# Conformer and differential attention trunk: PSUM banks, weight splits and read-backs of the attention stage

## What is computed

```python
q = (h @ w_q).reshape(B, S, N_HEADS, 2, HEAD_DIM)       # 8 heads, two halves of 64
for i in range(S // Q_BLOCK):                           # 8 query blocks of 128 rows
    end = (i + 1) * Q_BLOCK
    s = jnp.einsum("bqhcd,bkhcd->bhcqk", q_blk, k_pre) * scale
    p = jax.nn.softmax(s + bias[None, :, None], axis=-1)
    attn = p[:, :, 0] - lam * p[:, :, 1]
    outs.append(jnp.einsum("bhqk,bkhe->bqhe", attn, v_pre))
o = rmsnorm(o, subln_g) * (1.0 - lambda_init)
return o.reshape(B, S, V_WIDTH) @ w_o
```

## Time and profile before

| | |
|---|---|
| median of 3 runs | 2633.22 us (2631.69 to 2634.12) |
| profiled execution, its own time | 2629.98 us |
| its span | 2628.2 us |
| granted TensorE clock, mean | 0.972 |
| PE busy | 2425.7 us (92%) |
| DVE busy | 1477.3 us (56%) |
| ACT busy | 785.7 us (30%) |
| chain that ended last | PE 79%, DVE 15%, ACT 3% |

### The profile page before, as it was taken

How to read it: one execution, slowest core, us unless ns; L and a number is a source line. 1 busy time by engine, 2 the same in 40 slices (tenths; PEclk the granted TensorE clock), 3 DMA queues, 4 the chain that set the end, 5 groups by cost and what they waited for, 6 DMA issues and landing times.

```text
span 2628.2 us, 26809 instructions
## 1 busy us (share of the span) xinstructions
PE 2425.7 (92%) x10851; PEld 1929.7 (73%) x10851; DVE 1477.3 (56%) x2204; ACT 785.7 (30%) x1204; POOL 62.1 (2%) x51
## 2 busy tenths in 40 slices
PE   7995899999999999988888888679999999999997
PEld 5883688887777888866666666458688888888885
DVE  6998499895545344446766766653533333333233
ACT  5211432223434222234444444331421121121113
POOL 0000000000000000010111010000000000000000
PEclk9997899999999999999999999889999999999998
DMA  3110233332323333310111100211111111111111
GB/s 125 41 49 16 64 88 97 94 95 88 94 81 86 98 97 96 99 29 21 33 32 33 33 29 17 62 45 53 32 47 44 56 44 45 56 44 45 56 32 65
DMA packets 278297, 155.14 MB, mean 59 GB/s; under 512 B 5701, under 2 KB 273310, under 8 KB 278174
## 3 DMA queue, kind: packets, MB, share of 16 engines
q1 hardware_dynamic: 278174, 153.42, 19.6%
HBM read 145.54 MB, written 7.86 MB: 58 GB/s over the span
## 4 chain that ended last, share of the span: by engine, by line
PE 79%; DVE 15%; ACT 3%; issue 2%; DMA 1%; SPq 0%; DVEq 0%; ACTq 0%
PE ps L1333 25%; PE ps L1335 25%; PE ps L1334 24%; PE ps L1392 3%; DVE cacc L945 2%; DVE cvA L945 2%; PE ps L1316 2%; DVE rb L1182 1%; DVE sc L1161 1%; ACT sc L744 1%; DVE Wl L1107 1%; DVE sc L1159 1%; ACT ATh L757 1%; DVE sc L1146 1%; DVE Wl L873 1%
## 5 line engine op out<-in xcount | busy, mean ns | idle before, releaser
L1333 PE MATMUL ps<-Sh,Wl 128*128 128x512 f32 x2304 | 946.5, 411 | 87.3 <-DVE kS L1129 35.5
L1335 PE MATMUL ps<-Sh,Wh 128*128 128x512 f32 x2304 | 909.2, 395 | 0.0
L1334 PE MATMUL ps<-Sl,Wh 128*128 128x512 f32 x2304 | 908.6, 394 | 0.0
L1333 PEld LDWEIGHTS ps<-Sh,Wl 128*128 128x128 f32 x2304 | 439.0, 191 | 213.3 <-issue 105.5
L1335 PEld LDWEIGHTS ps<-Sh,Wh 128*128 128x128 f32 x2304 | 438.7, 190 | 94.6
L1334 PEld LDWEIGHTS ps<-Sl,Wh 128*128 128x128 f32 x2304 | 439.4, 191 | 93.5 <-issue 10.6
L873 DVE TENSOR_TENSOR Wl<-raw,Wh 128x1024 fp32r<-128x1024 f32 (+3 forms) x246 | 285.6, 1161 | 132.0 <-ACT Wh L566 130.9
L566 ACT ACTIVATE Wh<-raw 128x1024 fp32r<-128x1024 f32 (+3 forms) x246 | 245.7, 1002 | 321.2 <-PE ps L1335 159.7
L1057 DVE TENSOR_TENSOR xT<-ps,xT 128x512 f32<-128x512 f32 x112 | 77.2, 689 | 241.9 <-PE ps L1335 241.9
L757 ACT ACTIVATE ATh<-ps 128x512 fp32r<-128x512 f32 (+2 forms) x96 | 47.0, 489 | 311.8 <-PE ps L1316 311.7
L1050 DVE TENSOR_TENSOR tmp<-ps,rstd 128x512 f32<-128x512 f32 x66 | 45.6, 691 | 167.4 <-PE ps L1335 167.4
(11 more groups left out here) (161 smaller groups left out, 2686.0 us busy)
## 6 DMA issues: line engine op xcount, KB each, us to landing
raw<-in_ffn_w_dram SPq DMA_DIRECT2D x148, 512.0 KB, 3.8
raw<-in_pw_w_dram SPq DMA_DIRECT2D x32, 512.0 KB, 3.7
raw<-in_ffn_w_dram SPq DMA_DIRECT2D x32, 448.0 KB, 3.4
raw<-in_ffn_w_dram SPq DMA_DIRECT2D x24, 384.0 KB, 3.2
xrow<-in_x_dram SPq DMA_DIRECT2D x8, 512.0 KB, 7.6
raw<-in_w_q_dram SPq DMA_DIRECT2D x8, 512.0 KB, 3.7
raw<-in_w_k_dram SPq DMA_DIRECT2D x8, 512.0 KB, 3.8
raw<-in_w_v_dram SPq DMA_DIRECT2D x8, 512.0 KB, 3.6
```

The lines of the kernel that those rows point to most:

```text
L1333: pe.matmul(dst, ll, rh, start=start, stop=False)
L1334: pe.matmul(dst, lh, rl, start=False, stop=False)
L1335: return pe.matmul(dst, lh, rh, start=False, stop=stop)
```

## The change

Four things. The six projections of a head, and in head 7 the first seven output products, alternate between banks 0 and 1; each waits for the one two before it. All turns (transposes of weights and of V, sums of squares) go through bank 6, each waits for the one before it. Weight blocks are split one slot earlier: K and V of head h + 1 in rows 0 and 2, Q of head h + 2 in row 5, and Q of head 1 before the first scores. The read-back of results goes into `oback`, which lies exactly where `Sl` lies, so that no transfer waits for a buffer and the low part is written in place; the transfers begin when the last projection is done.

```diff
-TURN_BANKS = (6, 1)
+def row_parts(h, i):
+    table = LAST_FILL if h == HEADS - 1 else FILL
+    u = sum(map(sum, table[:i]))
+    for part in range(4):
+        if part == 1:
+            if i == 5:
+                yield ("o", h, 0), 0, 1
+            yield ("w", h, i, 0), 0, 1
+        if part == 2 and i < 2:
+            yield ("v", h, i), 0, 1
+        if part == 3:
+            if i == 0 and h:
+                yield ("o", h - 1, 1), 0, 1
+            if i >= 4:
+                yield ("w", h, i, 1), 0, 1
+        for n in range(table[i][part]):
+            yield projection(h, u)
+            u += 1
...
+def plan():
+    bank, before, holder = {}, {}, {0: None, 1: None, 6: None}
+    turn = 0
+    for key, step, _ in through_banks():
+        if step == 0:
+            bank[key] = 6
+            if key[0] in "pr":
+                bank[key] = turn % 2
+                turn += 1
+            before[key] = holder[bank[key]]
+            holder[bank[key]] = key
+    return bank, before
...
-        ostage = [qS, kS]
+        oback = at("oback", [P, 2, KC, HT], F32, S_AT + 32 * KB)
...
                 if h == HEADS - 1:
+                    sp.wait_ge(pj_mm, 6 * HEADS)
                     for k in range(HEADS - 1):
-
                         sp.wait_ge(o_out, 32 * (k + 1))
-                        if k < 2:
-                            sp.wait_ge(qk_lo, 4 * HEADS)
-                        else:
-                            sp.wait_ge(o_lo, k - 1)
-                        sp.dma_start(ostage[k % 2][:, :], o_dram[k]).then_inc(o_in[k % 2], 16)
+                        sp.dma_start(oback[:, :, k, :], o_dram[k].rearrange("p (a b) -> p a b", b=HT)) \
+                            .then_inc(o_in[k], 16)
...
                 if not last:
-                    if i in (0, 2, 4):
-                        att_split(h + 1, i // 2)
+                    if i in (0, 2):
+                        att_split(h + 1, K_R + i // 2)
+                    if i == 5 and h < HEADS - 2:
+                        att_split(h + 2, Q_R)
...
             att_split(0, V_R)
+            att_split(1, Q_R)
...
+            def bank_free(key):
+                b = BEFORE[key]
+                if b is None:
+                    pe.wait_ge(add_ok, 6 * KC)
+                elif b[0] == "p":
+                    pe.wait_ge(pj_ev, 6 * b[1] + (FIRST_ORDER.index(b[2]) if b[1] == 0 and b[2] < 4 else b[2]) + 1)
+                elif b[0] == "o":
+                    pe.wait_ge(ostd_ok, 2 * b[1] + b[2] + 1)
+                elif b[0] == "r":
+                    pe.wait_ge(wo_ev, b[1] + 1)
+                else:
+                    pe.wait_ge(tr_ev, SPLIT_TURN[b] + 1)
```

More of the change, by code:

```diff
@@ L145, with projection, through_banks @@
 LAST_DONE = [sum(map(sum, LAST_FILL[1:i + 1])) // (HEADS - 1) for i in range(TB)]
-def turns():
+MORDER = (5, 0, 1, 2, 3, 4)
+def projection(h, u):
+    if h == HEADS - 1 and u >= KC:
+        return ("r", (u - KC) // (HEADS - 1)), (u - KC) % (HEADS - 1), HEADS - 1
+    return ("p", h + (u >= KC), MORDER[u // KC]), u % KC, KC
+def row_parts(h, i):
[16 more added lines that the diff above has]
+            u += 1
+def through_banks():
+    for m in (0, 2, 1, 3, 4):
+        yield ("p", 0, m), 0, 1
     for h in range(HEADS):
         for i in range(TB):
[L152 to L169, removed]
-TURN_BANKS = (6, 1)
+            yield from row_parts(h, i)
+    yield ("o", HEADS - 1, 1), 0, 1
+def plan():
[10 more added lines that the diff above has]
+    return bank, before
+BANK, BEFORE = plan()
+SPLIT_TURN = {key: n for n, key in enumerate(k for k in BANK if k[0] in "wv")}
 VECS = {}
@@ L341, in trunk @@
         o_out = sem("o_out")
-        o_in = [sem(f"o_in{r}") for r in range(2)]
+        o_in = [sem(f"o_in{k}") for k in range(HEADS - 1)]
         o_hi = sem("o_hi")
@@ L747, in v_split @@
             def v_split(h, n):
[L748 removed]
+                key = "v", h, n
                 act.wait_ge(tr_mm, SPLIT_TURN[key] + 1)
[L750 removed]
+                act.activation(flat(Vh[:, 4 * n:4 * n + 4, :]), ps[:, BANK[key], :], ACT.Copy).then_inc(tr_hi, 1)
             def weights_split(h, i, n):
@@ L1246, in row @@
                 if not last:
-                    if i in (0, 2, 4):
-                        att_lo(h + 1, i // 2)
+                    if i in (0, 2):
+                        att_lo(h + 1, K_R + i // 2)
+                    if i == 5 and h < HEADS - 2:
+                        att_lo(h + 2, Q_R)
                     if i == TB - 1:
@@ L1558, in out_sum @@
             def out_sum(h, hf):
-                key = "o", h, hf, 0
+                key = "o", h, hf
                 pe.wait_ge(osq_ok, 2 * h + hf + 1)
-                turn_free(key)
-                pe.matmul(ps[:, turn_bank(key), :], ones[:, :], ob[:, :], start=True, stop=True).then_inc(ov_mm, 1)
+                bank_free(key)
+                pe.matmul(ps[:, BANK[key], :], ones[:, :], ob[:, :], start=True, stop=True).then_inc(ov_mm, 1)
             def out_free(j):
-                j0 = LAST_DONE[TB - 1]
-                if j <= j0:
-                    pe.wait_ge(*((wo_ev, j) if j else (pj_ev, 6 * HEADS)))
-                elif j <= j0 + 4:
+                if ("r", j) in BANK:
+                    bank_free(("r", j))
+                elif j < 2 * KC and ("r", j - 4) in BANK:
                     pe.wait_ge(s_ev, 2 * HEADS * TB)
@@ L1597, in fill @@
             def fill(h, i, part):
-                last = h == HEADS - 1
-                table = LAST_FILL if last else FILL
+                table = LAST_FILL if h == HEADS - 1 else FILL
                 u0 = sum(map(sum, table[:i])) + sum(table[i][:part])
                 for u in range(u0, u0 + table[i][part]):
-                    if last and i:
+                    key, k, _ = projection(h, u)
+                    if key[0] == "r":
                         out_product(u - KC)
                     else:
-                        q, k = u // KC, u % KC
-                        project(h + (q > 0), (5, 0, 1, 2, 3, 4)[q], k, k + 1)
+                        project(key[1], key[2], k, k + 1)
             def row(h, i):
```

68 lines of the change are left out of this document (26 added, 42 removed).

## The result

The changed kernel takes 2617.49 us (median of four runs, 2616.51 to 2618.36), the kernel before 2632.99 us (median of four): a ratio of 0.9941, with a 95% interval of 0.9924 to 0.9958. It is 15.5 us faster, clear of the noise, where 30.6 us were forecast. The profiled execution has a span of 2614.9 us against 2628.2 us, 13.3 us less, and a mean granted clock of 0.968 against 0.972.

The account below looks back on a forecast made before the run. PE's waits and slow clock were taken as the only time to win: -26.6 (rows 5 to 7) +5.4 +9 (rows 0 to 2) -2.4 (start) -16 (head 7) = -30.6, median 2603 us; own range 2595 to 2610, eight in ten 2588 to 2618.

Parts of the forecast that it names:

- +9: Rows 0 to 2, heads 1 to 6: lower clock behind the V stall, 1.55 us x 6, bounds 0 and +9.3.
- What bounds the kernel: Whole kernel: TensorE is busy 92% of the span; time is won only where PE stands or runs at lower clock.
- Rows 5 to 7: Each head's rows 5 to 7: K evacuation waits go, DVE and ACT set the pace; -3.65 us in heads 0 to 5.
- Row 7's wait: Before row 7's transposes: new wait about 2.5 us, slow clock still in three of seven heads; 0, bounds -5 and +6.
- V's transposes in row 1: Row 1, heads 1 to 7: V's transposes wait for bank 6's evacuation, a stall of 3.3 us.
- Early splits: Weight blocks split earlier: row 1's 1.2 us block wait goes; Q's block puts 1.05 us into the row 5 chain.
- Start: First projections and head 0: waits for evacuation, qS and part of the weight block's go; -2.4 us.
- Head 7: Last head: earlier read-backs -6.5 us, alternate banks for output products and full clock -9.5 us; together -16 us.
- Clock stays up: Rival: neither the V stall nor row 7's wait lowers the clock; 9 and 5 us less, 2589 us; chance 0.14.
- Read-backs land together: Rival, head 7: seven transfers share engines, the first landing with the last at about 1706; 2611 us; chance 0.12.
- Given back: Rival, rows 5 to 7: chain as long as the old waits, so heads win nothing; about 2615 us; chance 0.12.
- Slower: Rival: clock falls behind every short stall from one transposes bank, five slow stretches per head; 2651 us; chance 0.05.

Follow-up runs that it names:

- e1: Changed kernel with DVE's low part of row 1's weights ahead of the two reciprocals and the norm in heads 1 to 7; 2594.29 us.
- e7: Changed kernel with the weight blocks split where they were before the change (Q, K, V of the next head in rows 0, 2, 4); 2610.77 us.
- e6: Changed kernel with the read-backs through two staging buffers (qS and kS) as before the change; 2623.71 us.
- e4: Changed kernel with all projections and the first seven output products in bank 0 again, transposes in bank 6 alone; 2651.99 us.
- e12: e9 with read-backs taken up one row later in head 7 and row 7's projection steps as 3, 1, 1, 3; 2568.87 us.
- e9: e1 with sums of squares in a projection bank and four projection steps, not one, ahead of row 7's transposes; 2576.32 us.
- e5: Changed kernel with DVE's low part of row 1's weights between the two reciprocals; 2592.22 us.

## Why the prediction was right in sign and short in size

The 2617.5 us lie inside the range of 2588 to 2618, 0.5 us below its upper end, and outside the forecast's own range of 2595 to 2610. The four executions took 2616.5 to 2618.4, so that it lies inside and not outside is partly luck. The gains and losses stand where the prediction had them; their sizes were wrong, and all the large errors go the same way.

**A reading.** The two cycles of the earlier trace rows differ by 1.46 us (73.85 less 72.39), not by the 1.55 that the prediction took as the price of a slow stretch. In the six stretches of the +9 that is 0.5 us and changes nothing in what follows.

**What bounds the kernel** (right). Every wait that the prediction said would go is gone, and all the new ones stand where it put them: the root, the scores of rows 6, 7 and 1, the transposes of V. No further wait for bank 6 appeared in rows 0 or 4.

**Rows 5 to 7** (right in mechanism, too large). The chain on DVE and ACT was right to 0.4 us in its end, but its start came earlier too. In head 0, the one head without a slow stretch in either of the two pieces around it after the change, rows 5 to 0 take 35.1 us; heads before the change with one slow stretch there take 38.2. That is 3.1 us in place of 3.65, in six heads 3.3 us less than forecast.

**Row 7's wait, "three of seven: 0, bounds -5 and +6"** (wrong). It was sized by comparison with the old pair of waits, 1.50 and 1.35 us. The new single wait is 2.96 us, and a slow stretch follows in each of heads 1 to 5, in one of them a double one: six in the six heads where there were three. Single ones make rows 5 to 0 some 1.6 us longer (36.5 to 37.1 against 35.1). Three more give about +4.7. Together with the 3.3 us above this is nearly the 7.9 us by which the second row of the table was short. The upper bound of +6 held this term; the value taken did not. The window of head 0 from 1222.60 has 1.00 behind the same 2.96 us: of these six heads it was the one exception.

**V's transposes in row 1** (right in place and length, the clock's price too low). 3.54 us against 3.3. The "+9, bounds 0 and +9.3" let one slow stretch follow in each head. In four of six heads it was a double one, from 1247.84 in head 1 on, and rows 0 to 5 take 37.6 to 38.0 us there and 36.7 in the other two. The four give the 1.0 us each that is missing, and 0.2 us for the longer stall in every head the rest of the 5.3 us. The bound was wrong, since it held the stretch's length fixed. The trace shows what the four have in common: in them the clock fell 0.74 to 1.47 us before the stall's end, while PE still stood, and in the two single ones 0.28 us before its end or 0.21 us behind it. e1 shows the size of stall and clock together: 23.2 us.

**Early splits** (wrong). The prediction credited 1.2 us per head for the weight block's wait and charged the block's 1.05 us to the chain of row 6 separately. e7 shows the balance by a run: with both undone the idle time is the same to 0.6 us, and the kernel is 6.7 us faster. So a part of the change that was counted as a small gain is no gain in waits, and in this kernel it came with more time at the lower clock; that the split brings this by itself is not shown.

**Start** (-2.4, measured -0.8). The evacuation wait is gone. (Up to this sum e6 runs the same instructions as the changed kernel and is 0.9 us later there, so the piece is known to about 1 us.) But a stretch at 1.2 GHz now lies in the projection of V, whose eight steps last 7.3 us where 5.7 were counted on from before. One line of it on PE's timeline, where a product takes 0.63 us instead of 0.39:

```profile
1156.36 0.63 PE L1366 MATMUL ps<-Sl,Wh 128*128 128x512 f32 x1
```

**Head 7** (right, -16 against -15.1). e6 attributes 6.2 us of it to the read-backs, where 6.5 were forecast; e4, with its 10.8 us for the alternate banks under the output products, bears out the 8.3 to 9.5 us. The read-backs landed 1.35 to 1.75 us apart, where 1.45 was forecast, and 1.3 to 1.4 us later than forecast.

**Rivals.** "Clock stays up" fell. "Read-backs land together" fell: the first landed 4.6 us after its issue, 8.6 us before the last. "Given back" has a time near the measured one, 2615, but not the mechanism: the heads did win some 3 us each in rows 5 to 0 but for the clock, and it was the V stall and the clock behind it and behind row 7's wait that took them back. "Slower" named about the right price, 1.55 us per slow stretch (1.4 to 2.0 in rows 5 to 0), and the wrong count: 2.7 stretches per head were measured, and nearly five were needed. None followed the new waits of 0.9 us or less.

## What to carry to other kernels

A wait on the bounding engine has two prices, its own length and what the clock does behind it; taking away the stall of 3.54 us per head (e1) brought 13.4 us of idle time and 9.5 us of slower matmuls in six heads. So estimate both, with a doubled stretch as the upper bound. Where two resources are traded (two banks for one), list which engine empties the bank that is now shared and what stands ahead of that in its queue: moving one DVE instruction ahead of two reciprocals was worth more than the change itself. When the waits can't be removed, try moving work around them: that was worth 10.6 us and then 7.0 us here, the second with no less idle time. That full-size matmuls beside a wait are better than short ones is only suggested by one pair of kernels.

## What the runs showed of the hardware

The length of the longest wait alone did not decide the granted clock. In e12 a wait of 1.59 us with full transposes and projections beside it left it at 1.00 in all six heads of the profiled execution; in e9 a wait of 1.55 us among score products of 64 rows and 128 and 256 columns was followed by 0.5 in five heads. In the changed kernel 2.96 us (3.32 in head 5) was followed by it in five heads of six, and 3.54 us in six of six, for 6.8 us in four of them.

Nor did full-size products beside a wait protect the clock. Ahead of V's first projection PE waits 1.92 us in every version, with products of 512 columns on both sides. In the kernel before and in e4 the clock stayed up behind that wait; in the changed kernel and in e12 it fell, in e12 here:

```profile
1155.30 0.50 PE L1369 MATMUL ps<-Sh,Wl 128*128 128x512 f32 x1 [1.92 <-DVE Wl L1139]
...
1156.35 0.63 PE L1370 MATMUL ps<-Sl,Wh 128*128 128x512 f32 x1
```

The same wait among the same instructions can go either way from head to head. In e5, 2.96 us before row 7's transposes left the clock up in heads 0 and 1 and was followed by 0.5 in heads 2 to 4; in e7, the V stall of 3.3 us was followed by it in four heads of six. So a few heads of one trace are a small sample.

How long the clock stayed down went with the moment at which it fell. In the changed kernel's six heads the five stretches of 6.8 us began 0.74 to 1.47 us before the end of the wait; the six of 3.4 us began between 0.39 us before its end and 0.89 us behind it. In the same six heads of the other traces the double ones began at least 0.46 us before the end of the wait, the single ones at most 0.69.

Seven transfers of 512 KB from DRAM, issued one behind the other in 4.85 us, landed in the order of issue, the first 4.6 us after its issue and each further one 1.35 to 1.75 us behind the one before it.
